# The experts' stage: a loop of SyncE's own with one turn less, accumulators begun from x, the output gate folded in, norm and stores taken from PSUM

## The chip, the cores and the metric

The kernel runs on one core of a Trainium2 chip. The metric is the device time of one execution in microseconds, as the median of several runs. The engines are TensorE (PE, with its weight loads shown apart as PEld), VectorE (DVE), ScalarE (ACT), GpSimd (POOL) and SyncE (SP), which here issues nearly all transfers and computes nothing.

## The reference, cut to what matters

256 tokens of 1024 values go through two layers of a first block and one layer of a second block. The change touches only the end of the second block, a mixture of 32 experts of which each token uses four. In the reference:

```
    h2 = rmsnorm(x, norm2_w[layer]) * (1.0 + sc2) + sh2
    x = x + g2 * moe_ffn(h2, w_router, b_router, w_gate_up, b_gate_up, w_down, b_down)
return rmsnorm(x, final_norm_w)

# moe_ffn, for each token t and each of its four experts e, with w = softmax of the top four logits
    gu = x_t @ w_gate_up[e] + b_gate_up[e]          # 1024 -> 2048
    gate = min(gu[:1024], 7);  up = clip(gu[1024:], -7, 7)
    act = (up + 1) * gate * sigmoid(1.702 * gate)
    out_t += w * (act @ w_down[e] + b_down[e])      # 1024 -> 1024
```

`g2` is one row of 1024 values, the same for all tokens.

## The kernel before

All is float32. The 256 tokens are two tiles of 128 (`MT` = 2, index `m`), and outputs of 1024 columns are two halves of 512 (index `h`), each half one PSUM bank. What comes before the experts (the first block, the state-space mixer, the Fourier branch) is not touched.

**Router.** `pe_router` turns h2, makes the logits, and then begins the four accumulators (banks 4 to 7, one for each m and h) with four matmuls of zeros: `PT` and `yb`, both cleared by POOL, at L2497. `dve_router` finds the top four, ranks the tokens within each expert, and writes the number of rounds to `stat_i`: an expert takes 64 tokens (`SLOTS`) at a time, and the whole list of experts is walked once more for each further 64 tokens of the fullest expert. For these inputs it is one round. `pe_b_down` (L2509) turns the routing weights `W` to `WT`, 32 experts by 256 tokens, which ACT copies out of PSUM (L2541).

**The loop.** `experts` runs a loop over rounds and, inside, a loop over the 32 experts, on all five engines. Each engine keeps its own loop counter and they meet only through semaphores. In a turn PE multiplies with six weight chunks of 2 MB, each in a slot of its own (`slots`, three named ring, two named split, one named work): chunks 0 and 1 gate, 2 and 3 up, 4 and 5 down (`pe_pair`, L2683, eight matmuls each). Between them stand the biases (L2697), the scatter of the turn before (`pe_scatter`, L2673: each token gets the row of `yb` of its slot, added into the four accumulators, with the weight in `PT`), two kinds of turning (L2704, L2708) and the gather of the next expert's tokens (`pe_gather`, L2630). ACT copies the expert's output from bank 2 to `yb` at the turn's end (L2727). `yb` and `PT` of the last turn are scattered after the loop.

SP's part is `sp_expert` (L2624): for each q it waits until PE has used slot q (`w_used`), and issues the load of the next expert's chunk q. There are 32 turns and the first expert is loaded ahead of them by `sp_first_expert` (L2777), so the last turn loads an expert that nobody uses (a copy of expert 0 stands behind the list for it).

**The end.** `pe_end` adds the down biases, `WT` times `b_down`, into the four accumulators (L2824, all four matmuls read partitions 0 to 31), then the last scatter (L2831). `dve_end` takes each accumulator, multiplies by `g2` (L2851), and adds it to `x` (L2856). `act_end` squares and sums `x` (L2842). POOL makes the reciprocal root (L2810, L2812). DVE applies it and the row of `final_norm` to whole tiles of 1024 columns (L2862), and POOL issues the two stores of 512 KB (L2815). SP waits until the unused loads have landed (`sp_end`, L2797), and POOL for SP and for the stores.

## Time and profile before

| | us |
|---|---|
| median of 3 runs | 2687.61 |
| the runs | 2687.42, 2687.61, 2694.5 |
| span of the profiled execution | 2684.0 |
| own time of the profiled execution | not given; the median 2687.61 lies 3.6 above the span |
| PE busy | 2601.0 (97%) |
| DVE busy | 1078.7 (40%) |
| ACT busy | 878.5 (33%) |
| POOL busy | 93.2 (3%) |
| experts' loop, first to last matmul of it | 1729.5 to 2664.3 |
| end of the last turn's matmuls to the end of the span | 2664.3 to 2684.0 |

The span runs from the first to the last instruction of the profiled execution. Times in the rows are microseconds from its start. Busy time is no measure of what sets the end; for that there is the chain of waits, in which each step follows what released it.

### The profile page before, as it was taken

What the parts mean: (1) busy time and instruction counts of PE and PEld (TensorE: products, weight loads), DVE (VectorE), ACT (ScalarE), POOL (GpSimd) and SP (SyncE); (2) the same over time, 40 slices, a digit from 0 to 9 for tenths busy, and PEclk for the clock granted to TensorE, in tenths of its full rate; (3) what the DMA queues carried; (4) which work ended last, traced back from release to release, by engine and by line L of the source; (5) the groups of instructions that cost most, each with busy time, mean ns of one, the idle gap of its engine ahead of it and who ended that gap; (6) DMA issues with size and microseconds to landing.
All of it is one profiled execution on the core that took longest, in us unless ns stands there. A gap on an engine that the chain in (4) does not pass through costs nothing.

```text
span 2684.0 us, 31826 instructions
## 1 busy us (share of the span) xinstructions
PE 2601.0 (97%) x13026; PEld 1731.6 (65%) x13026; DVE 1078.7 (40%) x1681; ACT 878.5 (33%) x1389; POOL 93.2 (3%) x138
## 2 busy tenths in 40 slices
PE   7999989999999899999999999999999999999997
PEld 6887658878877678888888878644344344434433
DVE  4546454555555455466775645411111111111112
ACT  4435344444445244432234444311111111111111
POOL 0000200000002000000010000000000000000000
PEclk9999889999999899999999999999999999999999
DMA  6545545445546444342422234799999999999999
GB/s 254 188 177 189 193 180 188 184 181 188 188 178 233 190 188 183 126 181 104 157 95 78 80 135 160 280 412 425 428 428 429 428 428 429 428 428 429 428 429 418
DMA packets 51594, 700.86 MB, mean 261 GB/s; under 512 B 5890, under 2 KB 6034, under 8 KB 9104
## 3 DMA queue, kind: packets, MB, share of 16 engines
q1 hardware_dynamic: 48368, 687.80, 63.6%
q0 software_dynamic: 3136, 11.79, 1.3%
q8 instruction: 66, 1.08, 0.2%
q14 instruction: 24, 0.20, 0.0%
HBM read 696.43 MB, written 1.05 MB: 260 GB/s over the span
## 4 chain that ended last, share of the span: by engine, by line
PE 93%; DVE 3%; ACT 2%; DMA 1%; issue 1%; POOL 0%; SPq 0%; ACTq 0%; DVEq 0%
PE bank L398 40%; PE bank L2683 25%; PE bank L1723 7%; PE bank L2630 4%; PE bank L2697 2%; PE bank L2673 2%; PE bank L2034 1%; DVE split_r L375 1%; PE bank L2056 1%; ACT split_r L366 1%; PE bank L651 1%; DMA ring<-in_stream 1%; PE bank L958 1%; PE bank L1174 1%; PE bank L1104 1%
## 5 line engine op out<-in xcount | busy, mean ns | idle before, releaser
L398 PE MATMUL bank<-split_r,xT_r 128*128 128x512 f32 (+1 forms) x2880 | 670.9, 394 | 25.7 <-DVE split_r L375 12.0
L375 DVE TENSOR_TENSOR split_r<-ring,split_r 128x2048 fp32r<-128x2048 f32 (+1 forms) x200 | 458.0, 2291 | 506.1 <-ACT split_r L366 505.8
L398 PEld LDWEIGHTS bank<-split_r,xT_r 128*128 128x128 f32 x2880 | 543.4, 192 | 142.4 <-issue 24.2
L366 ACT CAST split_r<-ring 128x2048 fp32r<-128x2048 f32 (+1 forms) x200 | 379.1, 1896 | 531.2 <-PE bank L398 524.9
L398 PE MATMUL bank<-split_r,work_r 128*128 128x512 f32 x1920 | 461.1, 399 | 0.3 <-DVE split_r L375 0.3
L398 PEld LDWEIGHTS bank<-split_r,work_r 128*128 128x128 f32 x1920 | 358.9, 188 | 94.2 <-issue 7.4
L2683 PE MATMUL bank<-ring,work 128*64 128x512 f32 x1536 | 343.8, 597 | 1.7 <-DVE work L2647 1.7
L2683 PEld LDWEIGHTS bank<-ring,work 128*64 128x64 f32 x1536 | 107.9, 137 | 229.6 <-issue 229.6
L2683 PE MATMUL bank<-split,work 128*64 128x512 f32 x1024 | 232.2, 595 | 0.0
L1723 PE MATMUL bank<-work,ring 128*128 128x256 f32 x896 | 200.9, 379 | 0.0
L2733 DVE TENSOR_SCALAR work<-bank 128x512 f32<-128x512 f32 x32 | 22.1, 692 | 425.4 <-PE bank L2697 425.4
L1723 PEld LDWEIGHTS bank<-work,ring 128*128 128x128 f32 x896 | 166.9, 190 | 23.1 <-issue 1.0
L2683 PEld LDWEIGHTS bank<-split,work 128*64 128x64 f32 x1024 | 70.7, 137 | 130.1 <-issue 127.9
L2630 PE MATMUL bank<-work 128*128 128x64 f32 x1056 | 121.7, 273 | 0.5 <-DVE work L2654 0.5
L2630 PEld LDWEIGHTS bank<-work 128*128 128x128 f32 x1056 | 120.5, 192 | 0.7 <-DVE work L2654 0.7
L2735 DVE TENSOR_SCALAR work<-bank 128x512 f32<-128x512 f32 x32 | 22.1, 692 | 234.6 <-PE bank L2697 234.6
L2683 PE MATMUL bank<-work 128*64 128x512 f32 x512 | 115.3, 592 | 0.0
L1777 DVE SCALAR_TENSOR_TENSOR work<-bank,work 128x254 f32<-128x254 f32 x224 | 108.1, 482 | 8.0
L2722 ACT COPY work<-bank 128x256 f32<-128x256 f32 x32 | 11.9, 372 | 286.2 <-PE bank L2704 286.2
L2727 ACT COPY work<-bank 128x512 f32<-128x512 f32 x32 | 18.7, 585 | 240.7 <-PE bank L2683 240.7
L2720 ACT ACTIVATE work<-work 128x512 f32<-128x512 f32 x32 | 20.1, 629 | 218.0 <-DVE work L2733 218.0
L2683 PEld LDWEIGHTS bank<-work 128*64 128x64 f32 x512 | 36.8, 137 | 73.1 <-issue 73.1
(360 smaller groups left out, 1990.3 us busy)
## 6 DMA issues: line engine op xcount, KB each, us to landing
ring<-in_stream SPq DMA_DIRECT2D x224, 2048.0 KB, 9.1
split<-in_stream SPq DMA_DIRECT2D x66, 2048.0 KB, 14.8
work<-in_stream SPq DMA_DIRECT2D x33, 2048.0 KB, 13.5
ring<-in_stream SPq DMA_DIRECT2D x6, 1024.0 KB, 5.2
row<-in_rows POOLq DMA_DIRECT2D x6, 512.0 KB, 4.1
ring<-in_stream SPq DMA_DIRECT2D x2, 1120.0 KB, 6.1
work<-in_conv POOLq DMA_DIRECT2D x2, 768.0 KB, 5.6
x<-in_x SPq DMA_DIRECT2D x1, 1024.0 KB, 10.6
```

The source lines that it names most:

```text
L366: act.copy(hi, self.part(half)).then_inc(*up("half_hi", half.h))
L375: dve.tensor_tensor(lo, self.part(half), hi.bitcast(F32), ALU.subtract).then_inc(*(self.freed_up(half.chunk.c) if half.ends_chunk else up( ...
L398: mm = self.nc.tensor.matmul(out, a[x][a_at], w[y][w_at], start=start and n == 0, stop=stop and n == 2)
L651: tr = pe.transpose(self.bank[b][:, j * SEQ + m * P:j * SEQ + (m + 1) * P], self.hid[i % 2][:, m, (j2 + j) * P:(j2 + j + 1) * P], self.ident)
L958: mm = pe.matmul(self.bank[6][:, (4 * g + hh) * DK:(4 * g + hh + 1) * DK], self.pT[i % 2][:, hh, kb, :], self.z[:, kb, v0:v0 + DK], start= ...
L1104: mm = pe.matmul(bank[6][32 * kv:32 * kv + 32, 0:CMP_HIDDEN], self.xb[kv][:, j].rearrange("p a b -> p (a b)"), w[:, j, :], start=(j == 0), ...
L1723: mm = pe.matmul(bank[n % 2][:, 0:SEQ], w[:, k, j * P:(j + 1) * P], self.conv_src(n)[:, k, :], start=(k == 0), stop=(k == KD - 1))
L1777: dve.scalar_tensor_tensor(to, src[:, max(0, s):SEQ - max(0, -s)], wt[:, tap:tap + 1], to, ALU.mult, ALU.add).then_inc(*(up("tap", n) if t ...
L2630: mm = pe.matmul(bank[k // 4][:, k * SLOTS:(k + 1) * SLOTS], self.xs[:, m, k * P:(k + 1) * P], self.Pm[:, m, :], start=(m == 0), stop=(m = ...
L2673: mm = self.nc.tensor.matmul(self.bank[4 + 2 * m + h][:, :], self.PT[rows, m * P:(m + 1) * P], self.yb[rows, :], start=False, stop=stop)
L2683: mm = self.nc.tensor.matmul(self.bank[bank][h * SLOTS:(h + 1) * SLOTS, :], lhsT(k0 + k), w[:, k, h * 512:(h + 1) * 512], start=start and ...
L2697: mm = pe.matmul(bank[part][h * SLOTS:(h + 1) * SLOTS, :], self.sel[0:N_EXP, :], self.bias[0:N_EXP, part * D + h * 512:part * D + (h + 1) ...
```

## The change

Eight things are done together:

1. SP leaves the common loop and gets a flat loop of its own with `rounds * 32 - 1` turns, so that the unused expert is not loaded. POOL takes part in no loop. Nobody waits for unused loads at the end.
2. The four accumulators begin with `ident` times `x` in place of zeros.
3. `g2` is folded into what is added to them: into `yb`, by a multiply on DVE at the turn's end in place of ACT's copy, and into `b_down`, once before the loop.
4. For that `g2_rows` holds g2's left half on partitions 0 to 63 and its right half on 64 to 127, filled by two copies before the loop (`dve_expert_gain`).
5. `b_down` and `WT` are laid over four groups of 32 partitions, one for each m and h (`bias_rows`): four transfers in place of one, and four matmuls with columns 0 to 127 of bank 2 in place of two transposes.
6. After the loop nothing is multiplied or added on DVE before the norm: ACT squares the accumulators straight from PSUM, and DVE's last step reads them from PSUM, in halves.
7. The stores go out in four pieces of 256 KB, on SP.
8. PE waits for `b_gained` in place of `dma_b_down`.

The diff, cut to its core:

```diff
     def pool_router(self):
-        pool.dma_start(self.b_down[0:N_EXP, :], t["b_down"]).then_inc(*up("dma_b_down", 0))
+        for m in range(MT):
+            for h in range(2):
+                pool.dma_start(self.b_down[self.bias_rows(m, h), :], t["b_down"][:, h * 512:(h + 1) * 512]).then_inc(
+                    *up("dma_b_down", m, h))
...
-        pe.wait_ge(*at("zeros", 0))
         for m in range(MT):
             for h in range(2):
-                pe.matmul(bank[4 + 2 * m + h][:, :], self.PT[0:SLOTS, m * P:(m + 1) * P], self.yb[0:SLOTS, :], start=True,
+                pe.matmul(bank[4 + 2 * m + h][:, :], self.ident, self.x[:, m, h * 512:(h + 1) * 512], start=True,
                           stop=False)
...
         for m in range(MT):
-            tr = pe.transpose(bank[2][0:N_EXP, m * P:(m + 1) * P], self.W[:, m, :], self.ident)
+            for h in range(2):
+                tr = pe.matmul(bank[2][self.bias_rows(m, h), 0:P], self.W[:, m, :], self.ident, start=True, stop=True)
...
-        act.copy(self.WT[0:N_EXP, :], self.bank[2][0:N_EXP, 0:MT * P]).then_inc(*up("WT", 0))
+        act.copy(self.WT, self.bank[2][:, 0:P]).then_inc(*up("WT", 0))
...
         self.act_gather("next")
-        act.wait_ge(*at("w_used5", 0))
-        act.copy(self.yb, bank[2][:, :]).then_inc(*up("yb", 0))
...
         self.dve_gather("next")
+        dve.wait_ge(*at("w_used5", 0))
+        dve.tensor_tensor(self.yb, bank[2][:, :], self.g2_rows, ALU.mult).then_inc(*up("yb", 0))
...
-        with nc.Fori(0, rounds) as r:
-            with nc.Fori(0, N_EXP) as e:
+        with nc.Fori(0, rounds, engines=workers) as r:
+            with nc.Fori(0, N_EXP, engines=workers) as e:
                 s.loop(r * N_EXP + e)
-                self.sp_expert(e * 6 + 6, "next")
...
+        with nc.Fori(0, rounds * N_EXP - 1, engines=(nc.sync.engine,)) as turn:
+            s.loop(turn)
+            s.base = before
+            self.sp_expert(turn % N_EXP * 6 + 6, "next")
+            s.loop_end()
...
-        pe.wait_ge(*self.s.at("dma_b_down", 0))
+        pe.wait_ge(*self.s.at("b_gained", 0))
         for m in range(MT):
             for h in range(2):
-                pe.matmul(self.bank[4 + 2 * m + h][:, :], self.WT[0:N_EXP, m * P:(m + 1) * P],
-                          self.b_down[0:N_EXP, h * 512:(h + 1) * 512], start=False, stop=False)
+                rows = self.bias_rows(m, h)
+                pe.matmul(self.bank[4 + 2 * m + h][:, :], self.WT[rows, :], self.b_down[rows, :], start=False, stop=False)
...
-                act.activation(self.squares[:, 0:512], self.x[:, m, h * 512:(h + 1) * 512], ACT.Square, scale=D ** -0.5,
+                act.activation(self.squares[:, 0:512], self.bank[4 + 2 * m + h][:, :], ACT.Square, scale=D ** -0.5,
...
-            dve.scalar_tensor_tensor(self.end[:, m, :], self.x[:, m, :], self.stat[:, 12 + m:13 + m], self.row[:, :],
-                                     ALU.mult, ALU.mult).then_inc(*up("final", m))
+            for h in range(2):
+                cols = slice(h * 512, (h + 1) * 512)
+                dve.scalar_tensor_tensor(self.end[:, m, cols], self.bank[4 + 2 * m + h][:, :], r, self.row[:, cols],
+                                         ALU.mult, ALU.mult).then_inc(*up("final", m, h))
...
+                sp.wait_ge(*at("final", m, h))
+                sp.dma_start(t["out"][m * P:(m + 1) * P, cols], self.end[:, m, cols]).then_inc(*up("dma_out", m, h))
```

What stands in a row on PE around the start of the loop, before:

```order
L2491 MATMUL bank<-work 128x32 x2
L2497 MATMUL bank<-work 128x512 x4
L2501 MATMUL bank<-work 128x64
L2502 MATMUL bank<-work 128x32
L2503 MATMUL bank<-work 128x64
L2630 MATMUL bank<-work 128x64 x16
L2509 MATMUL bank<-consts,work 32x128 x2
L2782 TENSOR_LOAD stat_i
```

and now:

```order
L2499 MATMUL bank<-work 128x32 x2
L2504 MATMUL bank<-x,consts 128x512 x4
L2508 MATMUL bank<-work 128x64
L2509 MATMUL bank<-work 128x32
L2510 MATMUL bank<-work 128x64
L2638 MATMUL bank<-work 128x64 x16
L2517 MATMUL bank<-consts,work 32x128 x4
L2803 TENSOR_LOAD stat_i
```

The four accumulator matmuls stand where they stood, with other operands, and the turning of `W` has four matmuls for two.

On DVE the end of a turn of the loop and what follows the loop, before:

```order
L2647 TENSOR_SCALAR work<-bank,work,mod_T 128x64 x4
L2784 REGISTER_ALU
L2784 COMPARE_AND_BRANCH
L2783 REGISTER_ALU
L2783 COMPARE_AND_BRANCH
L2851 TENSOR_TENSOR work<-bank,cols 128x512 x2
L2856 TENSOR_TENSOR x<-x,work 128x512 x2
L2851 TENSOR_TENSOR work<-bank,cols 128x512 x2
L2856 TENSOR_TENSOR x<-x,work 128x512 x2
L2862 SCALAR_TENSOR_TENSOR work<-x,stat,row 128x1024 x2
```

and now:

```order
L2655 TENSOR_SCALAR work<-bank,work,mod_T 128x64 x4
L2749 TENSOR_TENSOR work<-bank,work 128x512
L2806 REGISTER_ALU
L2806 COMPARE_AND_BRANCH
L2805 REGISTER_ALU
L2805 COMPARE_AND_BRANCH
L2860 SCALAR_TENSOR_TENSOR work<-bank,stat,row 128x512 x4
```

The multiply by g2 is now one instruction in every turn, and eight instructions after the loop are gone.

On SP from the last load of a turn to the end, before:

```order
L2624 DMA work<-in_stream 128x4096
L2784 REGISTER_ALU
L2784 COMPARE_AND_BRANCH
L2783 REGISTER_ALU
L2783 COMPARE_AND_BRANCH
L2797 ISA
```

and now:

```order
L2632 DMA work<-in_stream 128x4096
L2812 ISA
L2812 COMPARE_AND_BRANCH
L2879 DMA out<-work 128x512 x4
```

The stores, which were `L2815 DMA out<-work 128x1024 x2` on POOL, now stand on the queue that loads the weights.

## Rows read from the trace of the kernel before

**Rows 1.** The page: shares of the chain that ended last, by engine.

```profile
PE 93%; DVE 3%; ACT 2%; DMA 1%; issue 1%; POOL 0%; SPq 0%; ACTq 0%; DVEq 0%
```

**Rows 2.** Windows: stretch, engines' busy us (count), granted clock, DMA share, GB/s.

```profile
1760.00:2664.00 904.00, 904.00 (x4654) 373.51 (x4650) 129.70 (x370) 147.06 (x279) 0.00 (x0) 1.00 1.01 428
1730.00:1732.00 2.00, 2.00 (x8) 0.65 (x6) 0.42 (x2) 0.16 (x1) 0.00 (x0) 0.52 0.00 0
```

**Rows 3.** Transfers issued in 1755:1785, then in 2640:2670: count, KB, median us to landing.

```profile
ring<-in_stream SPq DMA_DIRECT2D x3, 2048.0 KB, 12.1
...
ring<-in_stream SPq DMA_DIRECT2D x2, 2048.0 KB, 19.9
...
work<-in_stream SPq DMA_DIRECT2D x1, 2048.0 KB, 17.4
```

**Rows 4.** Timeline around a turn's end: start, us, engine, line, operands [idle before <-releaser].

```profile
1760.41 7.04 PE L2683 MATMUL bank<-ring,work 128*64 128x512 f32 x32
1760.63 0.58 ACT L2727 COPY work<-bank 128x512 f32<-128x512 f32 x1 [7.52 <-PE bank L2683]
...
1768.50 0.69 DVE L2733 TENSOR_SCALAR work<-bank 128x512 f32<-128x512 f32 x1 [13.47 <-PE bank L2697]
```

**Rows 5.** The chain ahead of the loop, in 1700:1745: start, us, what, count.

```profile
1718.83 3.63 PE bank L2497 x8
...
1729.51 8.78 PE bank L2683 x32
```

**Rows 6.** Timeline of ACT, PE and DVE ahead of the loop and in its first turn.

```profile
1716.59 1.07 PE L2486 MATMUL bank<-xT,work 128*32 128x256 f32 x16 [0.28 <-DVE xT L2551]
...
1727.41 0.38 PE L2509 MATMUL bank<-consts,work 128*32 128x128 f32 x2
...
1727.83 0.36 ACT L2541 COPY work<-bank 32x256 f32<-32x256 f32 x1 [0.71 <-PE bank L2509]
...
1739.35 0.69 DVE L2733 TENSOR_SCALAR work<-bank 128x512 f32<-128x512 f32 x1 [7.86 <-PE bank L2697]
```

**Rows 7.** Timeline of the tail.

```profile
2664.26 3.69 PE L2824 MATMUL bank<-work 32*128 32x512 f32 x8
2664.38 0.58 ACT L2727 COPY work<-bank 128x512 f32<-128x512 f32 x1 [7.52 <-PE bank L2683]
2664.52 0.33 SPq L2624 DMA_DIRECT2D work<-in_stream  x1
...
2667.89 1.99 PE L2831 MATMUL bank<-work 64*128 64x512 f32 x8
...
2669.07 1.29 DVE L2851 TENSOR_TENSOR work<-bank,cols 128x512 f32<-128x512 f32 x2 [10.61 <-PE bank L2831]
...
2673.39 0.63 ACT L2842 ACTIVATE work<-x 128x512 f32<-128x512 f32 x1 [0.86 <-DVE x L2856]
...
2675.03 0.94 POOL L2810 TENSOR_SCALAR stat<-stat 128x1 f32<-128x1 f32 x1 [0.65 <-ACT work L2842]
2676.05 0.56 POOL L2812 TENSOR_TENSOR stat<-stat 128x1 f32<-128x1 f32 x1
...
2676.73 1.28 DVE L2862 SCALAR_TENSOR_TENSOR work<-x,stat,row 128x1024 f32<-128x1024 f32 x1 [0.92 <-POOL stat L2812]
2678.31 0.53 POOL L2815 DMA_DIRECT2D out<-work  x1 [1.12 <-DVE work L2862]
```

**Rows 8.** Two matmuls on two column groups, in the timeline of a turn, and what follows.

```profile
1746.25 1.07 PE L2697 MATMUL bank<-work 32*64 32x512 f32 x4
1747.25 1.99 PE L2673 MATMUL bank<-work 64*128 64x512 f32 x8
```

**Rows 9.** Durations of POOL's same step after other norms (min/median/max ns), by line.

```profile
L469 POOL TENSOR_SCALAR stat<-stat x6: 217/219/418, 354.2 to 1716.6; 128x1 f32<-128x1 f32 x6
```

**Rows 10.** Transfers: the two stores' landing (line L2815); a 256 KB load issued at 1128.1.

```profile
DMA to landing us min/median/max: 5.7/5.8/5.8
...
DMA to landing us min/median/max: 2.7/2.7/2.7
```

More of the change, by code:

```diff
@@ L2420, in moe_views @@
         self.xs, self.squares, self.gate, self.silu = take(MT, D), take(D), take(512), take(512)
-        self.bias, self.b_down = take(2 * D), take(D)
+        self.bias, self.b_down = take(2 * D), take(512)
         self.xg, self.a, self.aT, self.yb = take(KD, SLOTS), take(512), take(4, 2, SLOTS), take(512)
@@ L2426, in moe_views @@
         at[0] = 14336
-        self.end, self.WT, self.W4, self.by_group = take(MT, D), take(MT * P), take(MT, TOP_K, N_EXP), take(SEQ)
+        self.end, self.WT, self.W4, self.by_group = take(MT, D), take(P), take(MT, TOP_K, N_EXP), take(SEQ)
         self.M, self.W, self.eq = take(MT, N_EXP), take(MT, N_EXP), take(MT, TOP_K, N_EXP)
@@ L2431, in moe_views, with bias_rows @@
         self.idx_u = take(MT, 8).bitcast(U32)
+        self.g2_rows = take(512)
+    def bias_rows(self, m, h):
+        return slice(64 * h + 32 * m, 64 * h + 32 * m + 32)
     def pool_router(self):
@@ L2790, in experts @@
                 s.loop_end()
-        self.turns = rounds * N_EXP
-    def sp_end(self):
-        for q in range(6):
-            self.nc.sync.wait_ge(*self.s.after_loop(f"dma_w{q}", ("next",), self.turns))
-        self.nc.sync.sem_inc(*self.s.up("weights_landed", 0))
+        with nc.Fori(0, rounds * N_EXP - 1, engines=(nc.sync.engine,)) as turn:
[3 more added lines that the diff above has]
+            s.loop_end()
     def pool_end(self):
```

60 lines of the change are left out of this document (31 added, 29 removed).

## The prediction

> **What bounds the kernel now.** I read the chain of waits first: PE is 93% of it [rows 1]. Then the windows: inside the experts' loop PE is busy 904.00 of 904.00 us at full clock, and no wait for a transfer appears [rows 2]. ACT's copy at a turn's end stands at 1760.63 and, 31 turns on, at 2664.38 [rows 4, 7], so a turn takes 903.75 / 31 = 29.15 us. Nothing in the change removes or adds a matmul inside a turn, so these 32 turns should stay; what can move is some 12 us ahead of the loop and 19.8 us behind it.
>
> The second thing that I looked at is how near the loads are to binding. In the loop the transfer engines are at 1.01 of their share, 428 GB/s [rows 2]. A 2 MB load of a ring slot lands 12.1 us after its issue in the second turn and 19.9 in the last but one turns [rows 3], some 7.8 us later over about 30 turns: the stream needs about 29.15 + 0.26 = 29.41 us for a turn and falls behind. A slot is needed again 29.15 - 3.5 (its own eight matmuls, half of 7.04 [rows 4]) - 0.14 (PE to issue, 2664.38 to 2664.52 [rows 7]) = 25.5 us after the issue. So even at the end 5.6 us are left at the median of the slots. PE is the bound, with a finite cover.
>
> The third is the tail. PE's last matmuls of the loop end at 2664.26. Down biases, 3.63 to the next group; last scatter, 1.18 to DVE's start at 2669.07; gain, add, squares, root, norm; the last store is issued at 2678.31 and lands 5.7 later [rows 7, 10], which is the end of the span, 2684.0. The unused load of the last turn, issued at 2664.52, lands at 2664.52 + 17.4 = 2681.9 [rows 3, 7]. So today it ends 2.1 us before the stores and is itself no bound.
>
> **Part by part: the loop and its cover.** SP without the last turn: nobody on PE waits for those loads, so by itself 0. It matters by what it clears: 12.6 MB are not in the way of the stores. If they were still there, stores on SP's own queue would stand behind a load that lands at 2681.9, and most of the gain below would go. SP's flat loop needs a remainder and two additions in each turn where it had a count; between the last issue of a turn and the first of the next lie slot 0's eight matmuls, 3.5 us, and 5.6 us of cover are behind that. Cost 0.
>
> The product with g2 on DVE: ACT's 0.58 [rows 4] becomes a DVE product of half a tile from PSUM, 0.65 (two in 1.29 [rows 7]). PE wants `yb` only behind four slots' matmuls of the next turn, 4 x 3.5 = 14 us later. Behind the new wait on DVE's queue stand the choice for the next turn and then L2733; before, L2733 waited 13.47 us for PE and started 7.9 us after ACT's copy did [rows 4], so it stays covered by about 6.8 us. Cost 0; without that cover 0.7 us in each turn.
>
> The fill of `g2_rows` and the gain of `b_down`, three DVE instructions of at most 0.65 to 0.69, so up to 2.1 us, once. They stand ahead of the loop on DVE's queue; L2733 of the first turn waits 7.86 us [rows 6]. Cost 0. Four small transfers on POOL's queue for one delay POOL by three issues of 0.53 to 0.63 [rows 7], 1.8 us at most; behind them on its queue stand the bias transfer and the clears, which nobody needs until the loop's start. Cost 0.
>
> **Ahead of the loop.** The four accumulator matmuls take 3.63 us, on the chain [rows 5]. With `ident` they are 8 rows of full height, as many as before, at the same 0.43 spacing; what falls away is going to a half-height array and back. The price of that is in the tail: eight rows of the 32-row form take 3.63 where 8 x 0.43 is 3.44. So -0.2 (bounds -0.4 and 0).
>
> Turning `W`: before two transposes span 0.38 [rows 6], now four matmuls of 128 columns, 8 rows in four column groups. The nearest row is L2486, 16 rows of 256 columns in four column groups in 1.07 [rows 6], 0.067 a row; 8 of them 0.5, plus a latency of 0.2: +0.3 (bounds 0 and +0.7). ACT's copy has 128 columns for 256, 0.36 to about 0.25: -0.1. PE reads the number of rounds behind this copy, so all three are on the path: sum 0.0, bounds -0.5 and +0.7.
>
> **The tail, step by step.** Start 2664.26 as before.
>
> Down biases: the four matmuls now sit in four groups of 32 rows and write four banks. L2673 shows that two row groups run beside each other: 8 rows take 1.99 against 3.69 in one group [rows 7, 8]; L2486 shows four column groups at once [rows 6]. Four row groups no row shows. If they all overlap, each group has two rows to run, like L2697, whose successor starts 1.00 later [rows 8]: -2.6. If only two do, as in L2673, about 1.9: -1.7. None: 0. I take -2.6, since four column groups did run at once. The Trainium skill, TensorEngine Tiling (Array Packing), Key Properties, says that different tiles can load weights and multiply in parallel, and that changing the tiling mode drains the engine; the first speaks for -2.6, the second is in the rows already, since there is a change of form at this place before and after.
>
> The scatter then starts at 2665.3. It needs `yb`, which DVE has at 2664.38 + 0.69 = 2665.07; covered by 0.2. The first tile's banks are complete 1.18 later, 2666.5 (from 2667.89 to 2669.07 [rows 7]). ACT can start there, where it started on x after DVE's gain and add.
>
> Squares: two took 1.64 from 2673.39 to POOL's start at 2675.03 [rows 7]. From PSUM ACT is a little faster (0.58 [rows 4] for 0.63 [rows 7]): 1.55. Second tile's follow at once: ACT is done, and POOL starts, at 2666.5 + 3.1 = 2669.6, against 2675.03: -5.4.
>
> Root on POOL: 0.94 and 0.56 before [rows 7]. The same step after other norms took 0.22 at the median, 0.42 at most [rows 9]. The slow ones ran beside DVE work that reads two tiles from SBUF (L2856, L2862); the new L2860 reads one of its two from PSUM. I take 0.22: -0.7 (bounds -0.8 and 0). The Trainium skill, SBUF — State Buffer, Who interferes with whom, says that a DVE instruction with two SBUF inputs contends with a GpSimd instruction that reads SBUF, and one with at most one does not. By that rule the 0.7 is gained; without it the sum would be 0.7 smaller.
>
> Norm: 1.28 for 1024 columns before; now two of 0.65, but the first half is stored while the second runs. 0.0 on the path. DVE's last end was 2676.73 + 1.28 = 2678.0; now 2678.0 - 5.4 - 0.7 = 2671.9.
>
> Stores: before 0.3 from DVE's end to the issue at 2678.31 on POOL and 5.7 to landing, 6.0. Now 0.1 and one piece of 256 KB on SP. The nearest row is a 256 KB load on SP's queue with nothing else under way, 2.7 [rows 10]; the upper bound is the store's 5.7. I take 2.7, since the old store had twice the bytes, POOL's own issue, and the unused load in the way until 2681.9: -3.2 (bounds -3.5 and -0.2). The Trainium skill speaks against a short landing: DMA: Bandwidth & Descriptors, Anatomy of one DMA, says that completion must wait for the write's receipt and that this can cause "a surprisingly long delay especially when the write target is HBM". Its fit of 2.0 us plus bytes over 436 GB/s would give an estimate of 2.6 for a piece.
>
> Sum behind the loop: -5.4 - 0.7 - 3.2 = -9.3, which holds the biases' -2.6. The end goes from 2684.0 to 2674.7. With 0.0 ahead of the loop and the 3.6 us outside the span (2687.6 less 2684.0, if the profiled run is like the median), the forecast is 2678.3 us.
>
> **Rivals.** (a) Shorter landing and parallel biases don't come: the pieces land after some 4.2 us and two row groups run at once. -9.3 + 1.5 + 0.9 = -6.9, 2680.7. For it: the receipt of a store is seen nowhere in isolation. Against: half the bytes, an idle queue.
> (b) It doesn't do what it says at the stores: another of SP's transfers is still under way. The last loads used are issued a turn earlier, before 2636, and land by about 2653, so nothing should be. With the old landing of 5.7 the sum is -6.3, 2681.3.
> (c) The clock. PE ran at half clock from about 1730 on, in the loop's first matmuls, after a mostly idle stretch [rows 2]; 32 rows took 8.78 for 7.04, so 1.7 us [rows 4, 5]. The longer turning of `W` fills part of that stretch. If the clock doesn't fall: -11.0, 2676.6; if it stays down for twice as long, -7.6, 2680.0.
> (d) Slower: the stream becomes the bound. Place: SP's own loop, whose arithmetic or release keeps the transfer engines empty for a moment in every turn. It decides when a turn of the stream takes more than 29.15 + 13.4 / 31 = 29.6 us (13.4 is 25.5 less the 12.1 of the second turn), 0.2 above today's 29.41. At 30.4 a turn, PE would wait 31 x 0.8 = 25 us in sum: 2687.6 - 9.3 + 25 = 2703. Against it: by the second turn transfers already queue behind each other, so a late issue of less than a microsecond leaves no hole.
>
> **How the numbers follow.** Forecast with small changes of its terms 0.62, (a) and (b) together 0.18, (c) 0.15, (d) 0.05. A measurement tells 0.3% from no change, 8.1 us, so the border is at 2679.5. Faster holds nearly all of the forecast and the faster half of (c), 0.70; same holds (a), (b), the slower half of (c) and the forecast's edge, 0.26; slower is (d) and a little, 0.04. The range takes in the bounds at the stores and the clock: 2675.5 to 2682.
>
> **What would show it.** Right: turns still 29.15 apart; no load by SP in the last turn; bias matmuls to scatter 1.0 us; ACT's first square 2.2 us after the loop's last matmul; POOL's steps 0.2 and 0.6; the last store landing 2.7 us after its issue; end 10.4 us after the loop. Wrong: PE waiting for a transfer in late turns; bias matmuls 0.43 apart; stores landing over 4 us; loop start later than 1730.

## The result: 18 us faster, twice what was forecast

| | before | changed |
|---|---|---|
| median, four runs each on one chip | 2687.52 (2681.9 to 2694.5) | 2669.05 (2667.12 to 2673.18) |
| ratio of the times, 95% | | 0.9931 (0.9914 to 0.9948) |
| mean of the runs on all chips | 2687.1 (86 runs, the four above not among them) | 2669.3 (16 runs, the four above among them) |
| span of the profiled execution | 2684.0 | 2665.6 |
| start of the down biases, behind the loop, to the end of the span | 19.8 | 9.8 |

The time lies 9.3 us under the forecast of 2678.3 and below the range that was given. Single runs of one kernel scatter with a standard deviation of mostly 3 to 5 us, so what follows compares means. The mean gain is 17.8 us, with a standard error of 1.0.

First the end, for which most of the working was done. From the page of the changed kernel, the chain of waits, shares of the span by engine:

```profile
PE 93%; DVE 3%; ACT 2%; DMA 1%; issue 1%; POOL 0%; SPq 0%; ACTq 0%; DVEq 0%
```

PE's share is the 93% of before [rows 1]; at this grain nothing is to be seen. The timeline of the changed kernel's end (start, duration, engine and line, out<-in, count, in brackets the idle time before and what ended it) answers [rows 7]:

```profile
2655.80 1.14 PE L2832 MATMUL bank<-work 32*128 32x512 f32 x8
...
2655.92 0.69 DVE L2749 TENSOR_TENSOR work<-bank,work 128x512 f32<-128x512 f32 x1 [5.93 <-PE bank L2691]
...
2656.87 1.99 PE L2838 MATMUL bank<-work 64*128 64x512 f32 x8
...
2658.05 0.60 ACT L2849 ACTIVATE work<-bank 128x512 f32<-128x512 f32 x1 [9.65 <-PE bank L2838]
...
2659.57 0.29 POOL L2869 TENSOR_SCALAR stat<-stat 128x1 f32<-128x1 f32 x1 [948.04 <-ACT work L2849]
...
2660.62 2.83 DVE L2860 SCALAR_TENSOR_TENSOR work<-bank,stat,row 128x512 f32<-128x512 f32 x4 [4.01 <-POOL stat L2871]
...
2661.07 0.29 POOL L2869 TENSOR_SCALAR stat<-stat 128x1 f32<-128x1 f32 x1 [0.56 <-ACT work L2849]
2661.40 2.41 SPq L2879 DMA_DIRECT2D out<-work  x4
2661.44 0.56 POOL L2871 TENSOR_TENSOR stat<-stat 128x1 f32<-128x1 f32 x1
```

L2832 are the down biases, L2838 the last scatter, L2849 the squares, L2869 and L2871 the root, L2860 the norm, L2879 the stores. From the biases (2655.80) the scatter comes 1.07 later, ACT's first square 2.25, POOL's first step for the second token tile 5.27, DVE's last end 7.65, and the end of the span, 2665.6, is 9.8 behind. The last of the four stores is issued at 2663.5 and lands 2.1 later; the tile of all four stores says so too:

```profile
DMA to landing us min/median/max: 2.1/2.1/2.1
```

The loop did not move. DVE's product with g2 (L2749), now the mark of a turn's end, stands in the first turn at

```profile
1752.17 0.69 DVE L2749 TENSOR_TENSOR work<-bank,work 128x512 f32<-128x512 f32 x1 [5.93 <-PE bank L2691]
```

and 31 turns on at 2655.92 in the rows above: 903.75 us, 29.15 a turn, as before. So the rest of the difference lies ahead of the loop. There, in the changed kernel's timeline, are the accumulator matmuls (L2504), the first of the counts (L2508), the turning of `W` (L2517), its copy, and the first matmuls of the loop:

```profile
1712.11 3.68 PE L2504 MATMUL bank<-x,consts 128*128 128x512 f32 x8
...
1715.62 0.33 PE L2508 MATMUL bank<-work 128*128 128x64 f32 x2
...
1720.64 0.43 PE L2517 MATMUL bank<-consts,work 128*32 128x128 f32 x8
...
1721.13 0.27 ACT L2549 COPY work<-bank 128x128 f32<-128x128 f32 x1 [0.88 <-PE bank L2517]
...
1722.75 7.09 PE L2691 MATMUL bank<-ring,work 128*64 128x512 f32 x32 [1.69 <-DVE work L2655]
```

The last row holds what the profile of before did not have: the loop's first 32 rows take 7.09 and not 8.78 [rows 5]. The windows of the same stretch (length; busy time and count of PE, PEld, DVE, ACT, POOL; granted clock; DMA share; GB/s) give full clock throughout:

```profile
1712.00:1716.00 4.00, 4.00 (x16) 2.09 (x15) 2.30 (x13) 2.08 (x6) 0.00 (x0) 1.00 0.91 379
1716.00:1722.00 6.00, 4.54 (x44) 4.07 (x43) 4.20 (x20) 1.56 (x5) 0.00 (x0) 1.00 0.03 14
1722.00:1732.00 10.00, 9.25 (x42) 2.96 (x44) 3.71 (x15) 1.67 (x2) 0.00 (x0) 1.00 0.45 159
```

**A trap in this pair of profiles.** Their spans differ by 18.4 us, about the measured gain, and their ends by 10.0. It is tempting to read the other 8.4 as the change's. But 6.6 us of it are there when the router starts, in code that is the same in both. The windows of the first 430 us, before and then changed:

```profile
0.00:430.00 430.00, 393.86 (x1974) 312.66 (x1975) 216.79 (x311) 186.13 (x281) 34.39 (x51) 0.95 0.53 198
```

```profile
0.00:430.00 430.00, 394.98 (x2013) 314.85 (x2014) 220.60 (x313) 190.01 (x282) 34.44 (x51) 0.98 0.54 201
```

The clock was 0.95 in one execution and 0.98 in the other, and the other did more in the same time (2013 rows of PE for 1974). In all the profiles here, 41 to 82 us of the first 1600 stand at half clock, partly in changing places. That these scatter the runs is likely; no run tests it. Two single profiles that agree with the measured difference can do so by chance; which part of the change earns what needed timed variants.

### The profile page after: what moved, and what is told of

Read it like the earlier page. It is cut to its first block, busy times and chain, and to the rows that moved or that the text cites. A ratio compares the mean times of both kernels' runs of the same rounds, so it can differ in the third digit from the quotient of the medians.

```text
span 2665.6 us, 31740 instructions
## 1 busy us (share of the span) xinstructions
PE 2589.2 (97%) x13032; PEld 1725.4 (65%) x13032; DVE 1097.5 (41%) x1710; ACT 860.0 (32%) x1357; POOL 92.5 (3%) x139
## 4 chain that ended last, share of the span: by engine, by line
PE 93%; DVE 3%; ACT 2%; DMA 1%; issue 1%; POOL 0%; SPq 0%; ACTq 0%; DVEq 0%
PE bank L398 40%; PE bank L2691 25%; PE bank L1723 7%; PE bank L2638 4%; PE bank L2705 2%; PE bank L2681 2%; DVE split_r L375 1%; PE bank L2056 1%; PE bank L2034 1%; ACT split_r L366 1%; PE bank L651 1%; DMA ring<-in_stream 1%; PE bank L1104 1%; PE bank L2716 1%; PE bank L958 1%
## 5 line engine op out<-in xcount | busy, mean ns | idle before, releaser
L2749 DVE TENSOR_TENSOR work<-bank,work 128x512 f32<-128x512 f32 x32 | 22.1, 692 | 189.7 <-PE bank L2691 189.7
```

## The experiments

Unless said otherwise an edit is made to the changed kernel, "gain" is the mean time of the kernel before on the same chip less that of the variant, with its standard error, and the changed kernel's own gain is 17.8. "Counts" is the time from the router's first index search for the top four on DVE to DVE's write of the number of rounds, "loop" that to the first turn's Silu on ACT. In the profile of the changed kernel they are 6.32 and 18.68, in that of before 6.62 and 20.58. Both start in the same place of the program, so they leave out what happened further up. Ratios are those that the runs came with; they differ a little from the quotient of the means. Single runs and single profiles are named as such.

### The changed kernel again

> The changed kernel once more, beside more runs of the kernel before. In the first traces the end came 18.4 us sooner in the span: 10.0 behind the loop, 1.7 of half clock in the loop's first matmuls, 0.2 ahead of the loop, and 6.6 in stages whose code is the same in both. Theory A (chance of the clock): the 6.6 are half-clock stretches that fall differently in every execution, so over more runs the mean granted clocks of both kernels overlap and the medians come to 12 to 15 us apart. Theory B (the change does it): the changed kernel keeps the higher clock, 0.985 to 0.989 against 0.982, in all runs, and the distance stays at 18 us or more. Time outside the span: 1.5 us in the changed kernel; if before has 3.5 in every run, 2 us of the gain stand there.

2670.8 us as a mean of 6, gain 17.2 ± 2.0, ratio 0.9929 (0.9909 to 0.9949). The size of the result stands. Neither theory holds as it was put: the mean granted clocks of single executions overlap (0.983 to 0.991 here, 0.979 to 0.986 before), as A had it, but the medians lie 17.7 apart, near B; outside the span 0.5 is gained and not 2. Its profile, with a span of 2675.8, shows how little one execution says: here the loop's start did have half clock, for 6.8 us, which moved it from 18.7 to 21.7 behind the router. Windows:

```profile
1722.00:1729.00 7.00, 5.78 (x49) 4.82 (x47) 3.95 (x19) 1.55 (x5) 0.00 (x0) 1.00 0.19 77
1729.00:1736.00 7.00, 6.05 (x16) 1.78 (x18) 3.25 (x15) 1.28 (x1) 0.00 (x0) 0.52 0.01 2
```

### SP's own loop alone, on the kernel before

```diff
-        with nc.Fori(0, rounds) as r:
-            with nc.Fori(0, N_EXP) as e:
+        with nc.Fori(0, rounds, engines=workers) as r:
+            with nc.Fori(0, N_EXP, engines=workers) as e:
                 s.loop(r * N_EXP + e)
-                self.sp_expert(e * 6 + 6, "next")
...
+        with nc.Fori(0, rounds * N_EXP - 1, engines=(nc.sync.engine,)) as turn:
+            s.loop(turn)
+            s.base = before
+            self.sp_expert(turn % N_EXP * 6 + 6, "next")
```

> Only SP's own loop with one turn less, POOL in no loop, no wait for unused loads; stores, gain, adds and norm as before. My prediction: PE and the chain are not touched, but the stores are no longer among the unused load's packets (their landing 5.7 before): the end 0 to 3 us sooner, 2685 to 2688 us. Rival: the unused load and the loop on POOL cost more than that, outside the span or in the stores: 5 us or more sooner.

2685.1 (12 runs), gain 2.8 ± 1.4, as expected; the ratio, 0.999 (0.9976 to 1.0004), takes in no change. POOL's stores of 512 KB landed in 5.8 behind the unused load [rows 10]; without it:

```profile
DMA to landing us min/median/max: 2.9/2.9/3.0
```

The tail is 1.86 shorter than before, although the landings are 2.8 shorter: here the clock fell to half at 2666.7, the last scatter took 3.66 for 1.99, and the stores were issued 0.9 later behind the loop. The last scatter ran at half clock in two more of the five profiles with the biases in one group (the one with the stores on SP, and `ident` times x alone), and in none of the thirteen with four groups. So the old landing of 5.7 was about half the unused load's doing. Turns stay 29.15 apart: the flat loop costs nothing.

Its profile held the case's main find. The accumulator matmuls (L2497, zeros, 64 rows high) and what follows them:

```profile
1712.42 5.25 PE L2497 MATMUL bank<-work 64*128 64x512 f32 x8
...
1719.43 7.09 PE L2630 MATMUL bank<-work 128*128 128x64 f32 x32 [0.29 <-DVE work L2654]
```

```profile
1714.00:1731.00 17.00, 14.96 (x51) 10.04 (x52) 6.56 (x33) 3.25 (x9) 0.00 (x0) 0.51 0.13 53
```

PE is at its lower level, 1.2 of 2.4 GHz, for 17.1 us, although it is busy 15 of them. The clock falls 2 us after the 64-row matmuls have begun. The gather (L2630), 3.79 us in the kernel with `ident` below, takes 7.09. Counts are 8.60 for 6.3, the loop 25.8 for 18.7 in the changed kernel.

### The same with the stores on SP

```diff
-        for m in range(MT):
-            pool.wait_ge(*at("final", m))
-            pool.dma_start(t["out"][m * P:(m + 1) * P, :], self.end[:, m, :]).then_inc(*up("dma_out", m))
...
+            self.nc.sync.wait_ge(*self.s.at("final", m))
+            self.nc.sync.dma_start(t["out"][m * P:(m + 1) * P, :], self.end[:, m, :]).then_inc(*self.s.up("dma_out", m))
```

> The edit of the run before, and the two stores of 512 KB on SP in place of POOL. If the issuing queue is what a store's landing costs: 2 us sooner than with the turn alone (landing 3.3 to 3.8 us for 5.7, issue 0.1 for 0.3), and time outside the span 1.5 for 3.5 if POOL's transfer at the end is what costs there. If HBM's write is what costs: landing stays above 5.

2683.6 (12 runs), gain 4.4 ± 1.5, which is 1.5 ± 1.7 more than above for the 2 that were expected, with the same 17.1 us of half clock ahead of the loop.

```profile
DMA to landing us min/median/max: 2.6/2.6/2.6
```

SP's landing is 0.3 shorter than POOL's and the issue takes 0.35 for 0.58: the tail is 0.6 shorter than in the kernel above. (Expected were landings of 3.3 to 3.8.) A further 0.5 comes from outside the span: the time less the span is 1.94 on average in the kernel before and 1.96 above, and 1.41 here. It goes with the queue that issues the stores (1.47 in the changed kernel, 2.02 in the variant with POOL's queue below).

### The unused expert loaded again

```diff
-        with nc.Fori(0, rounds * N_EXP - 1, engines=(nc.sync.engine,)) as turn:
+        self.turns = rounds * N_EXP
+        with nc.Fori(0, rounds * N_EXP, engines=(nc.sync.engine,)) as turn:
...
+        for q in range(6):
+            sp.wait_ge(*self.s.after_loop(f"dma_w{q}", ("next",), self.turns))
```

> The changed kernel with the unused expert loaded again (32 turns on SP) and SP waiting for it at the very end. The last unused load is issued some 0.3 us after the loop and lands 17 us later, as it did before. Theory of the prediction: the stores stand behind it on SP's queue, so they land after it, at 17 to 18 us behind the loop's end for 9.8 now: 7 to 8 us slower than the changed kernel, about 2676 us. Rival: stores go past it on the transfer engines: only 2 us slower in the landing, but the wait for the unused load still puts the end at 17.6 us.

2679.5 (12 runs), gain 8.4 ± 1.3, so 9.4 less than the whole change. The last load goes out at the loop's end and the stores queue behind it on SP:

```profile
2655.76 0.33 SPq L2632 DMA_DIRECT2D work<-in_stream  x1
2661.10 2.41 SPq L2880 DMA_DIRECT2D out<-work  x4
```

```profile
DMA to landing us min/median/max: 11.3/11.4/12.0
```

Issue is as early as in the changed kernel, landing 9.3 later at the median; the tail is 19.95 for 9.8. The last store lands at 2675.15, 2.5 behind the unused load (2672.61), so it is the store that sets the end. The turn less is worth 1.9 to 2.8 by itself and some 9 to 10 once the stores are on SP and early.

### The accumulators as before, on the changed kernel

```diff
+        pe.wait_ge(*at("zeros", 0))
...
-                pe.matmul(bank[4 + 2 * m + h][:, :], self.ident, self.x[:, m, h * 512:(h + 1) * 512], start=True,
+                pe.matmul(bank[4 + 2 * m + h][:, :], self.PT[0:SLOTS, m * P:(m + 1) * P], self.yb[0:SLOTS, :], start=True,
```

> The changed kernel with the four accumulators begun as before, with zeros on 64 rows (x is then left out of the sum; the output lacks it). In the profiles of the two kernels whose accumulators begin with zeros and that came with this study's first runs, the clock was at half for 17.1 us from the first of these four matmuls on; with x it was so for none, 3.4 and 6.8 us of the loop's start. Theory C (what the array multiplies there decides whether the clock holds): 4 to 8 us slower than the changed kernel's mean of 2670.3 us, 2674 to 2678. Theory A (chance of where the stretches fall): 2670 to 2672, only the 0.2 us of changing to half height and back. My prediction had 0.2.

2675.2 (12 runs), gain 12.4 ± 2.0: 5.4 less than the changed kernel. The same half clock appears, from 1715.3 on, for 17.1 us. Windows:

```profile
1713.00:1717.00 4.00, 4.00 (x11) 1.96 (x11) 2.29 (x13) 2.17 (x6) 0.00 (x0) 0.79 0.94 395
1717.00:1725.00 8.00, 7.71 (x30) 6.09 (x29) 2.93 (x15) 1.02 (x4) 0.00 (x0) 0.50 0.03 10
1725.00:1735.00 10.00, 8.35 (x40) 4.22 (x41) 4.27 (x18) 1.82 (x3) 0.00 (x0) 0.63 0.01 2
```

### Zeros, but 128 rows high

```diff
+        pe.wait_ge(*at("zeros", 0))
...
-                pe.matmul(bank[4 + 2 * m + h][:, :], self.ident, self.x[:, m, h * 512:(h + 1) * 512], start=True,
+                pe.matmul(bank[4 + 2 * m + h][:, :], self.PT[0:P, m * P:(m + 1) * P], self.yb[0:P, :], start=True,
```

> The same zeros, but on all 128 rows of the array (x left out). Separates height from data. If the zeros in the data cost the clock: as slow as the zeros on 64 rows, 2674 to 2678. If the half-height form does: as fast as the changed kernel, 2670 to 2672.

2671.7 (6 runs), gain 15.9 ± 1.8, not told from the whole change. No half clock:

```profile
1712.00:1716.00 4.00, 4.00 (x15) 2.09 (x14) 2.35 (x14) 1.86 (x5) 0.00 (x0) 1.00 0.93 390
```

### Data, but 64 rows high

```diff
-                pe.matmul(bank[4 + 2 * m + h][:, :], self.ident, self.x[:, m, h * 512:(h + 1) * 512], start=True,
+                pe.matmul(bank[4 + 2 * m + h][:, :], self.ident[0:SLOTS, :], self.x[0:SLOTS, m, h * 512:(h + 1) * 512], start=True,
```

> The first 64 rows of the unit matrix times the first 64 rows of x, on half the array's height (so each accumulator begins with half of x's tokens). The other corner of the same two factors. If zeros cost: 2670 to 2672 (with 0.2 for the form). If height costs: 2674 to 2678. If both count: between.

2677.2 (12 runs), gain 10.4 ± 1.4: 7.4 less than the changed kernel. Half clock for 17.1 us from 1720.0 on:

```profile
1722.00:1729.00 7.00, 6.71 (x28) 5.47 (x26) 2.93 (x15) 0.40 (x2) 0.00 (x0) 0.50 0.01 6
```

With the one above: between these forms it is the height that decides, not whether the numbers are zeros.

### `ident` times x alone, on the kernel before

```diff
-                pe.matmul(bank[4 + 2 * m + h][:, :], self.PT[0:SLOTS, m * P:(m + 1) * P], self.yb[0:SLOTS, :], start=True,
+                pe.matmul(bank[4 + 2 * m + h][:, :], self.ident, self.x[:, m, h * 512:(h + 1) * 512], start=True,
```

> The kernel before with nothing changed but these four matmuls: the unit matrix times x in place of zeros (x is then in the sum twice, once times g2). Theory C: 4 to 8 us faster than before's mean of 2688.0 us, 2680 to 2684. Theory A: 2687 to 2688.

2680.7 (12 runs), gain 6.9 ± 1.4; by the ratio, 0.9981 (0.9967 to 0.9994), 5 us, between 2 and 9. One line, and about a third of the whole. Full clock, counts at 6.32, loop at 18.61:

```profile
1714.00:1721.00 7.00, 4.77 (x41) 4.35 (x39) 4.83 (x25) 2.28 (x6) 0.00 (x0) 1.00 0.08 32
```

The runs without a profile bear the mechanism out too. Each run lists its span and mean granted clock, and 2 × (1 - clock) × span is the time that it spent at half clock. The mean of that is 93.5 us before and 76.8 here, 16.7 ± 3.7 less, about one stretch of 17.1. In the changed kernel it is 65.4; with 64-row zeros 79.4 and with 64-row data 84.7, 14.0 ± 5.7 and 19.3 ± 4.3 more. So the stretch is there in most executions with 64-row accumulator matmuls, though the profiled one of before happened to have only 3.4 us, later on.

What the clock did earlier goes with which it is. Some 36 us ahead of the router's search (32 for the shorter ones), in code that is the same in all, thirteen of the eighteen profiles have a stretch of 6.8 us at half clock (from 1676.7 in the changed kernel's). In the four of them with 64-row accumulator matmuls the 17.1 us follow; in the other nine the loop's start has full clock, but for the one below with two matmuls moved. Five profiles lack the 6.8 us. Three with nothing there (the kernel before, the unused expert, biases in one group) have 3.4 us at the loop's start, and two with 3.4 us there (the changed kernel again, DVE's product with one operand in PSUM) have 6.8. Among the first three the loop is at 20.58 with 64 rows and at 20.34 and 20.31 with 128: there the form costs 0.3 and not 7.1. Why the earlier stretch should matter no run shows.

### Biases in one group of rows again

```diff
-        for m in range(MT):
-            for h in range(2):
-                pool.dma_start(self.b_down[self.bias_rows(m, h), :], t["b_down"][:, h * 512:(h + 1) * 512]).then_inc(
-                    *up("dma_b_down", m, h))
+        pool.dma_start(self.b_down[0:N_EXP, :], t["b_down"]).then_inc(*up("dma_b_down", 0))
...
-            for h in range(2):
-                tr = pe.matmul(bank[2][self.bias_rows(m, h), 0:P], self.W[:, m, :], self.ident, start=True, stop=True)
+            tr = pe.transpose(bank[2][0:N_EXP, m * P:(m + 1) * P], self.W[:, m, :], self.ident)
...
-                pe.matmul(self.bank[4 + 2 * m + h][:, :], self.WT[rows, :], self.b_down[rows, :], start=False, stop=False)
+                pe.matmul(self.bank[4 + 2 * m + h][:, :], self.WT[0:N_EXP, m * P:(m + 1) * P],
+                          self.b_down[0:N_EXP, h * 512:(h + 1) * 512], start=False, stop=False)
```

> The changed kernel with the down biases as before: WT and b_down on partitions 0 to 31, two transposes of W, four matmuls in one group of rows. In the changed kernel the bias matmuls take 1.07 us to the scatter's start, and the end comes 9.8 us behind the loop. If the four groups of rows are what made it 1.07: 3.6 us here and the end 12.3 to 12.4 behind the loop. The turning of W: 0.38 for 0.43, copy 0.36 for 0.27: the loop's start within 0.1 us. If DVE's new product (0.69) would set the scatter's start anyway, less than 2.5 us are lost.

A single run, 2672.2 us. Its timeline shows the term by itself:

```profile
2658.28 3.69 PE L2827 MATMUL bank<-work 32*128 32x512 f32 x8
...
2661.90 1.99 PE L2834 MATMUL bank<-work 64*128 64x512 f32 x8
...
2663.08 0.60 ACT L2845 ACTIVATE work<-bank 128x512 f32<-128x512 f32 x1 [12.20 <-PE bank L2834]
```

3.62 from biases to scatter for 1.07 in four groups, and the end is 2.54 later, as expected. Four row groups do run at once.

### DVE beside POOL's root, from two SBUF tiles and from one

```diff
+        dve.wait_ge(*at("last_scattered", 1))
+        for j in range(3):
+            if j:
+                dve.wait_ge(*self.s.last("beside"))
+            dve.tensor_tensor(self.a, self.g2_rows, self.x[:, 0, 0:512], ALU.mult).then_inc(*up("beside"))
```

The second has `self.bank[2][:, :]` in place of `self.g2_rows`.

> The changed kernel with three DVE products of two tiles in SBUF (512 columns each) put between the last scatter and the norm, so that they run beside POOL's two steps for the first token tile. The Trainium skill, SBUF — State Buffer, Who interferes with whom: POOL's tensor_scalar takes 0.8 to 0.9 us as before, in place of the 0.29 of the changed kernel. Rival: POOL's 0.8 to 0.94 came from elsewhere (which operands ACT reads, or POOL waking from a long idle): 0.3 us here too. Nothing of the result changes.

> The same three DVE products, but one of the two operands is read from PSUM (bank 2). By the rule POOL's tensor_scalar stays at 0.3 us. If it takes 0.8 here as well, any DVE work beside it does it.

First with both operands in SBUF, then with one in PSUM:

```profile
2665.71 2.15 DVE L2859 TENSOR_TENSOR work<-work,x 128x512 f32<-128x512 f32 x3 [2.37 <-PE bank L2838]
...
2666.30 0.29 POOL L2874 TENSOR_SCALAR stat<-stat 128x1 f32<-128x1 f32 x1 [948.01 <-ACT work L2849]
...
2666.68 0.87 POOL L2876 TENSOR_TENSOR stat<-stat 128x1 f32<-128x1 f32 x1
```

```profile
2665.17 2.14 DVE L2859 TENSOR_TENSOR work<-bank,x 128x512 f32<-128x512 f32 x3 [2.37 <-PE bank L2838]
...
2665.76 0.29 POOL L2874 TENSOR_SCALAR stat<-stat 128x1 f32<-128x1 f32 x1 [951.00 <-ACT work L2849]
...
2666.14 0.56 POOL L2876 TENSOR_TENSOR stat<-stat 128x1 f32<-128x1 f32 x1
```

Beside two SBUF operands POOL's power takes 0.87 for 0.56, beside one it is not slowed, and its first step takes 0.29 in both. In the first variant the power starts at 2666.68, while DVE's second product runs, and ends at 2667.55, 0.4 into the third; 0.3 is added to this step. It does not move the end: in both variants the third product sets the norm's start, and the tail is 10.15 and 10.14 for 9.8. The first step, at 2666.30, met only the last 0.1 of the first product and was not slowed. So the slowing is shown for the power (0.85 and 0.56 in the kernel before); for the first step, which the expectation named and which took 0.80 and 0.94 there, it stays an inference. The rival of a POOL slow after a long idle time is refuted: in the changed kernel that step takes 0.29 after 948 us. The Trainium skill, SBUF — State Buffer, Who interferes with whom, names just this pair (DVE with two SBUF inputs, POOL reading SBUF), and the trace agrees with 0.87 against 0.56. The single times, 2674.3 and 2673.4, can't tell so small a thing.

### The stores on POOL

```diff
     def sp_end(self):
-        sp, at, up, t = self.nc.sync, self.s.at, self.s.up, self.t
+        sp, at, up, t = self.nc.gpsimd, self.s.at, self.s.up, self.t
```

> The changed kernel with the four stores of 256 KB issued by POOL in place of SP. In the changed kernel the last is issued 0.1 us after DVE and the span ends 1.9 us after the issue; with the two stores of 512 KB on SP and no unused load (second run of this study) a store landed in 2.9. If POOL's issue is what the old landing cost: 1.5 to 2.5 us slower (0.5 to 0.6 for each issue, four of them behind each other, and a longer way to the first packet), and 1.9 us outside the span for 1.5. If the unused load was all of it: the same as the changed kernel within 0.5 us in the span.

2674.7 (11 runs), gain 10.5 ± 1.3; by the means 5.4 to 7.3 slower than the changed kernel, for the 1.5 to 2.5 that were expected. (The 2.9 that the expectation names is a store on POOL in the second run; on SP it was 2.6.)

```profile
DMA to landing us min/median/max: 2.4/2.8/3.0
```

Issues of 0.54 to 0.64 on POOL for 0.34, and landings of up to 3.0 for 2.1, make the tail 1.23 longer; outside the span 0.5 is added. That explains 1.7 of the 7.3 by which the gain is smaller. This chip's runs of before are 1.9 faster than the mean of all, and compared with the changed kernel's absolute mean 5.4 are lost. The mean time at half clock is 78.2 ± 2.4 us for 65.4 ± 2.9; the edit touches nothing on PE, and no run here shows why. No runs of the changed kernel are known to be from this chip, so a difference of chips is not ruled out. SP is the better queue; 1.7 of its worth is understood.

### Both halves of the array, 64 rows at a time

```diff
+        pe.wait_ge(*at("zeros", 0))
+        for again in range(2):
+            for m in range(MT):
+                for h in range(2):
+                    rows = slice(h * SLOTS, (h + 1) * SLOTS)
+                    pe.matmul(bank[4 + 2 * m + h][:, :], self.PT[rows, m * P:(m + 1) * P], self.yb[rows, :],
+                              start=not again, stop=False)
```

> The kernel with zeros on 64 rows (x left out of the sum), but eight matmuls in place of four, alternating between rows 0 to 63 and rows 64 to 127, so that two run beside each other in the same form: the same 3.5 us, the same 64-row form, but both halves of the array at work. Theory C1 (the array half idle is what lets the clock fall): loop's start as with x on all rows, mean 2670 to 2672. Theory C2 (the 64-row form does it, or changing to it and back): half clock for 17.1 us as before, 2675 to 2677.

2669.9 (6 runs), gain 16.5 ± 2.0. Twice the matmuls, in the 64-row form, alternately on the upper and the lower half, take the 3.7 us of the 128-row form, and the clock stays:

```profile
1717.56 3.70 PE L2507 MATMUL bank<-work 64*128 64x512 f32 x16
```

```profile
1717.00:1721.00 4.00, 4.00 (x20) 1.98 (x20) 2.30 (x13) 2.44 (x6) 0.00 (x0) 1.00 0.94 394
1721.00:1728.00 7.00, 5.22 (x48) 4.55 (x46) 4.50 (x22) 1.70 (x6) 0.00 (x0) 1.00 0.07 26
```

Counts are 6.62, as in the profile of before, and the loop 19.00: at full clock the form costs 0.3. So neither the form nor the change between forms brings the half clock: the clock fell where half of the array had nothing to do, and held where both halves worked.

### Can the accumulators be begun in PE's idle time?

The counts wait for the accumulator matmuls. Here two of the four, and then one, are moved behind the turning of `W`:

```diff
-        for m in range(MT):
-            for h in range(2):
-                pe.matmul(bank[4 + 2 * m + h][:, :], self.ident, self.x[:, m, h * 512:(h + 1) * 512], start=True,
-                          stop=False)
+        for m, h in ((0, 0), (0, 1), (1, 0), (1, 1))[0:2]:
+            pe.matmul(bank[4 + 2 * m + h][:, :], self.ident, self.x[:, m, h * 512:(h + 1) * 512], start=True,
+                      stop=False)
...
         tr.then_inc(*up("W_turned", 0))
+        for m, h in ((0, 0), (0, 1), (1, 0), (1, 1))[2:4]:
+            pe.matmul(bank[4 + 2 * m + h][:, :], self.ident, self.x[:, m, h * 512:(h + 1) * 512], start=True,
+                      stop=False)
```

> The changed kernel with its two accumulator matmuls of the second token tile moved behind the turning of W, into the time in which PE waits for ACT's copy and the number of rounds. PE's 3.68 us ahead of the counts were 1.06 us longer than DVE's way to them (DVE done with its reduce at 14.63 in the changed kernel's span of that stage, PE at the counts at 15.62): 0.9 to 1.0 us sooner at the counts, the moved 1.7 us fit in the gap of 1.7 before the loop, or cost up to 0.5 there. In the changed kernel's profiles half clock struck the loop's first matmuls after this gap in 4 of 7 (1.7 or 3.0 us each); if a filled gap keeps the clock, another 1 us in the mean. Sum: 0.5 to 2 us faster than the changed kernel. Rival: PE reads the number of rounds only when its matmuls are done, and the loop starts 1 us later.

> Only one of the four moved. 0.8 us sooner at the counts, 0.86 us of the gap filled: 0.5 to 1 us faster than the changed kernel; if the rival of the run before holds, this one loses nothing.

> The changed kernel once more, on the chip of these three, as their base: 2669 to 2672 us.

On one chip: 2670.9 (6 runs, two moved), 2670.9 (7 runs, one moved), 2667.7 (6 runs, the changed kernel). Counts come 0.84 sooner in both (5.47 and 5.48 for 6.31), and with one moved the loop too, 17.83 for 18.64. With two moved the profile had half clock again ahead of the loop, from 1723.0 on, and the loop at 21.20:

```profile
1723.00:1730.00 7.00, 7.00 (x32) 5.45 (x32) 3.47 (x22) 2.52 (x6) 0.00 (x0) 0.51 0.00 0
...
1721.56 5.79 PE L2640 MATMUL bank<-work 128*128 128x64 f32 x32 [0.52 <-DVE work L2664]
```

The gather (L2640), 3.8 us elsewhere, is where the clock fell, 3.5 us after the two full-height matmuls that were left and before the moved ones ran. So idle rows are not the only thing that a fall can follow here: half as many full-height matmuls at this place were followed by one too, in one profile.

No gain can be measured, and both are 3.2 us slower than the changed kernel, by 1.6 to 2 standard errors. The expected 0.5 to 2 did not come. The changed kernel stays the fastest that was found; its ratio here is 0.9931 (0.9912 to 0.9951).

## Where the prediction was right and where it failed

| term | forecast | found | from |
|---|---|---|---|
| loop, 31 turns | 0 | 0.0 | 903.75 in every profile |
| behind the loop | -9.3 | -10.0 | the two tails |
| outside the span | 0 | -0.5 | means of time less span |
| accumulator form | -0.2 | -5 to -8 | -6.9 ± 1.4 alone, 5.4 and 7.4 when undone |
| turning of `W` and its copy | +0.2 | 0.0 | loop at 18.61 and 18.64 to 18.68 without and with it |
| sum | -9.3 | -15.5 to -18.5 | measured -17.8 ± 1.0 |

**What bounds it, the loop and its cover**: right. PE sets every turn, the flat loop of SP costs nothing, and the slower rival (d), a stream that falls behind, did not come.

**The tail**: right in its mechanism and close in each step. Biases to scatter 1.07 (forecast 1.0), and undoing the four groups cost 2.54 (forecast 2.6). DVE's last end 7.65 behind the loop (forecast 7.64). POOL's steps 0.29 and 0.56 (forecast 0.22 and 0.56). Only the stores were mis-sized: 2.1 to landing where the nearest row, a load of as many bytes, had 2.7, which makes the store term -3.9 for -3.2. The estimate of 2.6 by the fit of the Trainium skill (DMA: Bandwidth & Descriptors, Anatomy of one DMA, where it stands for GpSimd's path) is above it too; on POOL's queue the same pieces took 2.4 to 3.0. The receipt of a write to HBM that the page warns of is within the 2.1, and no run here splits it off. Rivals (a) and (b) took longer landings, and are both refuted. The price put on the removed turn, "most of the gain below would go", is right: 9.4 went, of the 10.0 behind the loop, for stores 9.3 later. One thing the tail of before hid: with its biases in one group the last scatter ran at half clock in three of five profiles, which put the stores 0.7 and 0.9 later in the two that can be compared. If that is so in most executions, the tail's mean gain is up to 0.9 above the 10.0; no timed variant shows it.

**The time outside the span** was not 3.6. It is 1.9 on average before, so the profiled execution was most likely some 1.7 faster than the median. As it was added to both sides this cost nothing, but a difference was hidden in it, the 0.5 of SP's queue.

**The step that failed** is "Ahead of the loop", its first sentence: going "to a half-height array and back" was priced at 0.2 in all, from the tail, where eight rows of the 32-row form took 3.63 for 8 times 0.43. At full clock that is about right: 0.3 by the counts. What the term left at nothing is what the clock does after half of the array has idled: 17.1 us at half clock, 7.1 on the path, in most executions, and so 5 to 8 us in the mean for the 0.2. Rival (c) did have the clock, and its stretch of half clock at the loop's start exists. But it looked there only, where the one profile of before showed it, behind idle time of PE, and not at the 17.1 us, which came with PE busy for 15 of them; hence its size, 1.7 either way.

Could it have been seen? Only in part. The profile of before has half clock for 3.4 us behind this stretch and none in it, among some 97 us in all (2 × (1 - 0.982) × 2684): it was of the kind that has no 6.8 us ahead of the router. What could have been asked is why the mean granted clock was 0.982, and what each stretch at half clock followed. A cause with a varying effect would have widened the range downwards.

**What stays open.** Why the variant with POOL's stores lost 3.7 to 5.6 us more than its tail and its outside time explain. Why five of the thirteen profiles without idle rows still have 3.4 to 6.8 us of half clock at the loop's start or just ahead of it, and why that, like the 17.1 us, goes with what the clock did some 36 us ahead of the router's search. And how the stretches further up, 41 to 82 us in all, come about; they are the largest thing left outside the loop.

## To carry to other kernels

Price a matmul by what the granted clock does behind it as well as by its own row: matmuls that leave half of the array idle cost 0.3 us here at full clock and 5 to 8 us in the mean by what followed, and the full-height form took the same 3.7 us. Before removing a transfer that "nobody waits for", ask what it will stand in front of once the end comes sooner: the unused load was worth 1.9 to 2.8 us alone and over 9 with early stores on its queue. And with a scatter of 3 to 5 us between runs, time each part of a change by itself; a pair of profiles gave the right sum here with a wrong split.

## What the hardware showed that was not expected

- After 64-row matmuls (eight rows of 512 columns) the clock went to half for 17.1 us in four of five profiles, with PE busy 15 us of it; after 128-row ones, or 64-row ones on both halves in turn, it fell while they ran in none of thirteen. Zeros or data made no difference that these runs tell (gains of 12.4 ± 2.0 and 10.4 ± 1.4 with 64 rows). The 17.1 us came only where 6.8 us at half clock stood some 36 us ahead of the router's search.
- Stores of 256 KB landed in 2.1 us on SP's idle queue, where a load of that size had 2.7, and stores of 512 KB in 2.6; on POOL's queue it was 2.4 to 3.0 and 2.9.
- Stores on POOL's queue rather than SP's add 0.5 us outside the span of instructions.
- Four matmuls in four groups of 32 rows, writing four banks, let the next group of matmuls start after 1.07 us, for 3.62 in one group.
